# Other start addresses for the four summed activation tiles of a seven-product feed-forward layer

## The reference, cut to what matters

```python
def swiglu(x, w_in, w_out):
    gu = x @ w_in                      # [512, 1024] @ [1024, 2 * 2816]
    g, u = gu[..., :D_FF], gu[..., D_FF:]
    return (jax.nn.silu(g) * u) @ w_out
...
x = layer_norm(ALPHA * x + 0.5 * swiglu(x, ffn_w_in[l, 0], ffn_w_out[l, 0]), ln_g[l, 0], ln_b[l, 0])
```

## Time and profile before

| | us |
|---|---|
| median of 3 runs | 3254.2 |
| lowest, highest | 3250.09, 3259.59 |
| the profiled execution | 3251.48 |
| its span | 3249.7 |
| PE busy (share of the span) | 3157.5 (97%) |
| DVE busy | 2143.2 (66%) |
| ACT busy | 1535.2 (47%) |

### The profile page before, as it was taken

How to read it: one execution, slowest core, us unless ns; L and a number is a source line. 1 busy time by engine, 2 the same in 40 slices (tenths; PEclk the granted TensorE clock), 3 DMA queues, 4 the chain that set the end, 5 groups by cost and what they waited for, 6 DMA issues and landing times. The chain is left out here.

```text
span 3249.7 us, 58922 instructions
## 1 busy us (share of the span) xinstructions
PE 3157.5 (97%) x24214; PEld 2863.2 (88%) x24214; DVE 2143.2 (66%) x3383; ACT 1535.2 (47%) x2651; POOL 137.5 (4%) x144
## 2 busy tenths in 40 slices
PE   9999999999999999999999988999999989999999
PEld 9998998999889988779998877879998867789997
DVE  7875544788577856448875766557874665667863
ACT  4553444355435543644553544444554444444553
POOL 0000111000000001000000100000000000000000
PEclk9999999999999999999999999999999999999999
DMA  4343222234323332112433221113332211123332
GB/s 180 143 141 110 95 72 90 76 136 148 117 88 127 134 121 93 53 66 88 143 134 123 86 72 60 37 63 117 131 142 97 99 66 53 41 83 119 141 126 72
DMA packets 104523, 331.73 MB, mean 102 GB/s; under 512 B 11264, under 2 KB 16640, under 8 KB 104256
## 3 DMA queue, kind: packets, MB, share of 16 engines
q1 hardware_dynamic: 104256, 327.96, 28.7%
HBM read 325.69 MB, written 2.23 MB: 101 GB/s over the span
## 5 line engine op out<-in xcount | busy, mean ns | idle before, releaser
L222 DVE TENSOR_TENSOR wlo<-raw,whi 128x1024 fp32r<-128x1024 f32 x319 | 387.7, 1224 | 433.3 <-ACT whi L214 432.6
L214 ACT ACTIVATE whi<-raw 128x1024 fp32r<-128x1024 f32 x319 | 334.2, 1055 | 386.4 <-PE ps L379 333.5
L803 PE MATMUL ps<-tz,whi 128*128 128x256 f32 x1728 | 477.6, 276 | 3.4 <-ACT tmp L975 3.4
L804 PE MATMUL ps<-tz,whi 128*128 128x256 f32 x1728 | 477.1, 276 | 0.0
L805 PE MATMUL ps<-tz,wlo 128*128 128x256 f32 x1728 | 477.1, 276 | 0.0
L241 PE MATMUL ps<-xh,whi 128*128 128x256 f32 x1424 | 410.3, 288 | 18.4 <-DVE wlo L222 11.1
L377 PE MATMUL ps<-whi,tz 128*128 128x512 f32 x1056 | 412.1, 390 | 0.0
L379 PE MATMUL ps<-whi,tz 128*128 128x512 f32 x1056 | 411.0, 389 | 0.0
L378 PE MATMUL ps<-wlo,tz 128*128 128x512 f32 x1056 | 410.9, 389 | 0.0
L243 PE MATMUL ps<-xh,wlo 128*128 128x256 f32 x1424 | 397.9, 279 | 0.0
L242 PE MATMUL ps<-xl,whi 128*128 128x256 f32 x1424 | 397.7, 279 | 0.0
(11 more groups left out here) (348 smaller groups left out, 6509.2 us busy)
## 6 DMA issues: line engine op xcount, KB each, us to landing
raw<-in_w SPq DMA_DIRECT2D x535, 512.0 KB, 3.7
fb<-in_w SPq DMA_DIRECT2D x108, 256.0 KB, 2.5
rows<-in_row SPq DMA_DIRECT2D x15, 512.0 KB, 4.6
xr<-in_xt SPq DMA_DIRECT2D x4, 512.0 KB, 6.6
xr<-in_x SPq DMA_DIRECT2D x1, 2048.0 KB, 7.4
mn<-bounds SPq DMA_DIRECT2D x8, 256.0 KB, 4.6
out<-tmp SPq DMA_DIRECT2D x4, 256.0 KB, 3.5
out<-rows SPq DMA_DIRECT2D x4, 256.0 KB, 2.3
```

Of the source, the lines that this page charges most:

```text
L214: a.activation(self.whi[u % NW][:, :], self.raw[u % NRAW][:, :], COPY).then_inc(*self.up("whi", u))
L222: v.tensor_tensor(self.wlo[u % NW][:, :], self.raw[u % NRAW][:, :], f32(self.whi[u % NW][:, :]), SUB).then_inc(*self.up("wlo", u))
L803: t.matmul(out, fh[:, sl], xh[:, k, :], start=first and k == 0, stop=False, skip_group_check=not first)
L804: t.matmul(out, fh[:, sl], xl[:, k, :], start=False, stop=False, skip_group_check=not first)
```

## The change

Each of the eight parts of the sums gets a slot of 4352 bytes (4096 and 256 more, so that all slots begin at the same place modulo 256), and within the slots of sum q its parts begin `BEGIN[q]` words in: 16, 32, 224 and 240 bytes. With `tz` at 64 modulo 256, T1 begins at 80, T2 at 96, T3 at 32 and T4 at 48, high and low parts alike. `tz` grows from 32832 to 34816 bytes per partition, so `es` and `fb` behind it move by 1984 bytes, from 128 to 64 modulo 256. The `fed` slots stay where they were; they now overlap other parts of the sums, and `split_a` waits accordingly: for products 2, 2, 6, 6, 7, 7, 4, 4 in its first eight steps, where it waited for 2, 6, 6, 7, 7, 4, 4, 4. No instruction is added, removed or moved on any engine, and every instruction waits on the same semaphores as before; addresses differ, and the values of some of these waits.

```diff
+SLOT = 2 * T + 4 * LINE
+BEGIN = {1: 4, 2: 8, 3: 56, 4: 60}
...
-        q = 2 * int(name[1]) - 2
-        return [blocks(self.tz[:, 2 * T * (q + i):2 * T * (q + i + 1)], HT) for i in range(2)]
+        q = int(name[1])
+        at = [SLOT * (2 * q - 2 + i) + BEGIN[q] for i in range(2)]
+        return [blocks(self.tz[:, a:a + 2 * T], HT) for a in at]
...
-                a.wait_ge(*c.at("prod", s, KF - 1, (2, 6, 7, 4)[min((m + 1) // 2, 3)]))
+                a.wait_ge(*c.at("prod", s, KF - 1, (2, 6, 7, 4)[m // 2]))
...
-            hf, tz = c.sb("hf", [P, KF, T], F32, scope), c.sb("tz", [P, 8 * 2 * T + LINE], F32R, scope)
+            hf, tz = c.sb("hf", [P, KF, T], F32, scope), c.sb("tz", [P, 8 * SLOT], F32R, scope)
```

## The result

The changed kernel takes 3279.2 us (median of 4 runs, 3278.1 to 3283.3), the kernel before 3256.1 (median of 4 runs on this occasion, 3250.1 to 3259.6). The ratio is 1.0067, with a 95% interval of 1.0046 to 1.0088: slower by 15 to 29 us. The profiled execution took 3278.67 us with a span of 3276.9, that is 27.2 us more span than before. Forecast were 3254 us and no change.

A forecast was written before the change was run, and what follows sets the result against it. The prediction took PE's matmul spacing as the bound. All terms were 0, so 3251.5 + 0 = 3251.5 us against the profiled execution; with the median of runs 2.7 us higher, it forecast 3254 us, range 3240 to 3298.

The forecast's parts named there:

- What bounds the kernel: Whole kernel: PE is busy for 97% of the span, so only the spacing of its matmuls can move the time.
- The price of the start address: 5184 matmuls on the four sums: new starts off 64 cost 0, bounded by -26 and +37 us.
- The bounds of -26 and +37 us: Sums' 5184 matmuls: at best the transposes' 108 ns spacing, at worst one further 64-byte piece, 7.1 ns each.
- The line rule: Moving operands in SBUF: lines of 16 bytes, each new line priced; new starts keep 64 lines per matmul, so 0.
- The wide spacing on the sums alone: Rival, products on the sums: they fall into the wide spacing, 4.4 ns a matmul, +23 us, 3274 to 3277; chance 0.13.
- The price for a piece of 64 bytes: Rival, sums' matmuls: a start off 64 bytes touches a 17th piece, 7.1 ns each, +37 us, 3291 us; chance 0.13.
- The faster rival: Rival, sums' matmuls: another distance modulo 256 escapes the extra 6.6 ns, -26 us, 3228 us; chance 0.13.
- The other terms: Writes of the sums by ACT and DVE, shift of `es` and `fb`, later waits of the splitting: each 0, hidden by slack.
- The chances: Whole kernel: no change of spacing 0.52; measured slower by over 0.3% 0.34, faster 0.13, within 0.53.

The follow-up runs named there:

- the sweep by types: Model left out, bare matmuls timed over sixteen moving starts, stationary at 128: bfloat16 109.2 ns, float32 215.8 at all; float32r 113.3 at 64 and 240, 116.7 to 120.0 elsewhere.
- the bare kernels: Four kernels that leave the model out and time blocks of 36 or 48 matmuls at chosen start addresses; moving 64 beside stationary 128 took 113.3 or 117.8 ns.

## Why the prediction was wrong, point by point

**What bounds the kernel** held. Only PE's spacing moved; the waits, DVE's room and the second product stayed. The reading that the trace holds a narrow and a wide spacing, 113.3 and 117.7 ns, for the same operands held too, and both were met again in five more kernels, whose heads ran at 113.4 to 113.9 ns in some layers and at 117.6 to 117.8 in one to three others.

**The price of the start address** is the step that failed. It was taken as 0 from the float32 matmuls on `mv`, called the nearest row. It isn't near, and the prediction had called it mild and taken it even so: the sweep by types shows float32 flat over all sixteen starts where float32r is not. The term measured 54 to 65 ns per product of a sum, 4.5 to 5.4 ns a matmul, 26.0 us over the trace. The bounds of -26 and +37 us contained it.

**The missing term** is the product that follows. A sum's price was laid on its own 5184 matmuls; the next product on `xh` pays 12 or 22 ns as well, 3.5 us over the trace.

**The line rule** of the Trainium skill, page "SBUF — State Buffer", section "Door 1: The DMA port swizzle", was weighed for the zero. By it, starts at multiples of 16 bytes should be alike. The measurement decides against reading it so: sixteen such starts gave spacings from 113.3 to 120.0. It doesn't speak of two streams, and the argument took it further than it goes.

**The rivals.** The wide spacing on the sums alone was priced at +23 us and 3274 to 3277 us and given 0.13; the chip gave +27 in the trace and 3279. It is the one that came true, in place and nearly in size, and with its sign: the matmuls on `tz` last 281 to 282 ns and step by about 118. It was short by two things: the starts used have spacings of their own, 117.8 to 118.8 in the products and not the 117.7 of the fallen-out rhythm, and the followers. "It comes and goes with no change of address" stood against it; that was true of start 64 and was wrongly taken to mean that addresses don't matter. What it meant is that 64 beside 128 is one of the two moving starts of sixteen that reached 113.3 in any block. The price for a piece of 64 bytes fell: the four starts cost 4.5 to 5.4 ns and not 7.1, and 0, 128 and 192, which need no further piece, pay as well. The faster rival fell: 113.3 is the least that float32r showed in any of its pairs with 256 columns; the 109.2 ns that the prediction estimated from the 262 clocks of the Trainium skill, page "TensorE: Matmul & The Clock Gate", section "Back-to-back issue gap", are what bfloat16 takes here, to the tenth.

**The other terms** of 0 (the writes of the sums, `es` and `fb`, the waits) held: with the old starts in the new slots the ratio is 0.9993, and what is left of them is within its interval.

**The chances.** The row that should have moved them was in front of me: the kernel's moving operands all stand at 64 with weights at 128, or at 128 with 128, and where the roles are turned round, 128 beside 64, the same trace has 229 ns and more where 226.7 is possible. That was a pair of distances with different spacings, in the trace of before, and it wasn't read.

## What to carry to other kernels

Where TensorE is the bound and works in float32r, the start addresses of both operands modulo 256 are worth up to 6% of a matmul of 256 columns (113.3 to 120.0 ns over multiples of 16): read the spacing of starts, not the duration, by operand pair, and compare it with the least that the trace shows for that shape. Move the two operands together or not at all; change the start between products as seldom as possible; and mind that a tensor that is moving in one stage and stationary in another can't be at its best in both. A row of another type is no bound for this one.

## What the runs showed of the hardware

- float32r, 256 columns, stationary at 128: 113.3 ns at moving starts 64 and 240, 116.7 to 120.0 at the fourteen others; bfloat16 109.2 and float32 215.8 at every start.
- Moving both operands by 32 bytes changes nothing (113.4 ns), moving one of them by 32 costs 5 ns on each matmul (118.3).
- The spacing has a memory. The same operands run at 113.3 or at 117.8 ns for hundreds of matmuls, and what came before decides. In the trace of before the second head fell to 117.8; with the new slots and the old start it was the whole last layer, with the shift by 32 the whole last layer and the first head. A layer's part costs 6.7 us. Single runs of one kernel differ by about as much (3250 to 3260 us), but that such falls make the difference was not shown, and there is a second candidate: in the kernel with all moving operands at 240, where no part fell in the trace, the twelve runs go from 3253.7 us at a mean granted clock of 0.996 to 3260.0 at 0.993. The first 144 matmuls of two of the bare kernels are the same instructions and ended at 113.3 ns in one and 117.8 in the other. What sets it at a restart stays open.
- A change of start costs the first 2 to 12 matmuls 1 to 17 ns each, also between two starts that are good by themselves (127 and 130 ns for the first two of T1 at 240).
